# A two-layer encoder step on one core: the passages between dense blocks taken by token halves

## The chip, the core and the metric

The kernel runs on one core of a Trainium2 chip. The metric is the device time of one execution in microseconds (us). TensorE does the matmuls, VectorE and ScalarE read its results from PSUM and do the element-wise work, GpSimd takes a little of that, and SyncE issues most DMAs. In the profile's rows they are PE, DVE, ACT, POOL and SP; PEld is TensorE's weight load.

## What is computed

One inference step of two layers over 656 token columns (16 meta tokens and 512 prompt tokens, then 8 streams of 16). Each layer is, cut to what matters:

```python
h = rmsnorm(x, norm_mix_pre)
mix = token_mixers(h)                     # one input projection, attention and HGRN2 heads, one output projection
x = x + rmsnorm(mix, norm_mix_post)
h = rmsnorm(x, norm_ffn_pre)
u = h @ w_ffn_up                          # 1024 -> 2 * 2816
f = (silu(causal_conv3(u[:, :2816])) * u[:, 2816:]) @ w_ffn_down
x = x + rmsnorm(f, norm_ffn_post)
```

and after the second layer `y = rmsnorm(x, final_norm)`. Everything is float32; beside y, caches and states are returned.

## The kernel before

Activations lie transposed: features on 128 partitions, the 656 tokens along a row, and D = 1024 features are `KD` = 8 chunks `X[:, k, :]`. A PSUM tile has two banks; a tile's result puts tokens 0 to 327 into the first (half 0, or A) and 328 to 655 into the second (half 1, or B). There are four PSUM tiles: `G[0]` and `G[1]`, which dense tiles use in turn (tile number tt goes to `G[tt % 2]`), and `WA` and `WB`, which attention and the norms use.

**Dense products.** To keep float32 accuracy, every operand is split into a high and a low part (`Hh`, `Hl` of activations, `whi`, `wlo` of weights), and a product is three matmuls. `tile()` makes one output tile of 128 features: 8 chunks (11 for the down projection) of 3 matmuls for each half, so 48 or 66 matmuls of 328 columns. Weights come as a stream of pieces of 128x1024: SyncE loads a piece into one of two raw buffers, `w_high` on ScalarE and `w_low` on VectorE split it into one of three slots, and a slot is free when the last tile that used it has ended (`piece_end`).

**Passages.** Between two dense blocks lies a passage: the norm over all features needs the last tile, the residual needs the norm, and the next block needs the new X. There are three between blocks (layer 0's output projection into FFN, layer 0's FFN into layer 1's input projection, layer 1's output projection into FFN), and one at each end of the kernel. In a passage of before, with all 656 tokens at once:

- the squares of the last tiles are added up in `acc` by VectorE (`add_square`), TensorE adds over partitions by a plain float32 product with `ones` (`norm_sum`), and ScalarE makes the factor `R` (`rstd`: Ln and Exp);
- for each chunk k, VectorE writes tmp = Y * gain * R (`residual`, L1178 to L1188), GpSimd adds it to X (L317 to L321), ScalarE writes `Hh` and the square of X (`split_x`, L832 to L837), VectorE writes `Hl` (`rest_of_x`, L1167 to L1170), and TensorE does chunk k of the next block's first tile and, by `ones`, of the sum of squares (`square_sum`, L399 to L410);
- the norm before the block isn't applied to X: the factor `R` of that norm is multiplied into the tiles when VectorE reads them from PSUM. So the first tiles can run before that `R` is known, but can't be read.

Every engine has one instruction queue, worked off in the order in which it is written, and semaphores carry the dependences between engines; `tile_free(tt)` makes TensorE wait until the tile two before has been read. In FFN two up tiles make one unit: the gate tile in G[0] (times R, convolution, silu) and the value tile in G[1] (times R and the gate). FFN's first up tile is number 0 here; a block's fourth tile, tile 3, goes to G[1], which tile 1 must have left.

## Time and profile before

| what | value |
|---|---|
| time, median of 3 runs | 2143.87 us (2143.34 to 2146.22) |
| the profiled execution's own time | 2142.33 us |
| its span | 2140.5 us |
| TensorE busy | 1990.0 us, 93% |
| VectorE, ScalarE, GpSimd busy | 1144.7, 714.7, 167.7 us |
| mean granted TensorE clock | 0.946 of full speed |

The busy time of TensorE is a modelled one (its matmuls are pipelined), and the span is that of one execution, 1.8 us below its own time. Busy shares are averages over stages with different limits; a passage is read from the timeline.

### The profile page before, as it was taken

Reading aid. Unit: us, or ns where it says so; the run is one execution under the profiler, and the core shown is the slowest. Engines: PE = TensorE matmul, PEld = TensorE weight load, DVE = VectorE, ACT = ScalarE, POOL = GpSimd, SP = SyncE. Lnnn points to the kernel's source line nnn. Section 1 sums busy time; section 2 is a strip of 40 time slices with the busy share of each in tenths; the row PEclk is TensorE's granted clock in tenths of the full one; section 3 lists DMA queues with packets and bytes.
Section 4 is the critical chain, followed back from the end, with each engine's and each line's share of the span. In section 5 each row is a group of like instructions: output and inputs, shape, how many; then the busy total and the mean of one; then the engine's idle time right before and its main releaser. Section 6 shows DMA issues by size and latency. Waiting matters only on the chain.

```text
span 2140.5 us, 30609 instructions
## 1 busy us (share of the span) xinstructions
PE 1990.0 (93%) x12316; PEld 1803.3 (84%) x12316; DVE 1144.7 (53%) x1819; ACT 714.7 (33%) x1064; POOL 167.7 (8%) x145
## 2 busy tenths in 40 slices
PE   7999989899799999999799999898988999999995
PEld 6988866469699999999788888564787999999993
DVE  4777754332666515664456778452237663266535
ACT  4444334233422222222243444352234222222222
POOL 0000032300200000000100001332001000000002
PEclk9999988889899999999898999797999999999997
DMA  5111130131122222222121111302121222222211
GB/s 181 56 51 61 61 82 1 45 109 50 33 80 79 70 79 70 70 79 70 53 84 46 51 61 60 72 1 89 64 70 52 70 70 79 70 79 70 79 51 54
DMA packets 42045, 141.83 MB, mean 66 GB/s; under 512 B 4961, under 2 KB 6881, under 8 KB 41889
## 3 DMA queue, kind: packets, MB, share of 16 engines
q1 hardware_dynamic: 33248, 117.51, 16.8%
q10 hardware_dynamic: 8656, 22.37, 3.3%
q8 instruction: 98, 1.61, 0.3%
q14 instruction: 43, 0.34, 0.0%
HBM read 130.13 MB, written 8.65 MB: 65 GB/s over the span
## 4 chain that ended last, share of the span: by engine, by line
PE 78%; DVE 12%; ACT 7%; issue 1%; DMA 1%; ACTq 0%; SPq 0%; DVEq 0%; POOLq 0%; POOL 0%
PE G L384 62%; PE WA L384 8%; PE WB L384 5%; DVE tmp L1124 2%; DVE Hl L1124 2%; PE G L388 2%; DVE Y L1124 2%; DVE DE L1124 1%; ACT sq L800 1%; PE WB L388 1%; DVE Z L1124 1%; DVE wlo L1124 1%; ACT Y L800 1%; ACT whi L800 1%; ACT tmp L800 1%
## 5 line engine op out<-in xcount | busy, mean ns | idle before, releaser
L384 PE MATMUL G<-Hh,wlo 128*128 128x328 f32 x2304 | 742.6, 322 | 49.7 <-DVE Hl L1124 49.1
L384 PE MATMUL G<-Hh,whi 128*128 128x328 f32 x2304 | 728.7, 316 | 0.0
L384 PE MATMUL G<-Hl,whi 128*128 128x328 f32 x2304 | 722.1, 313 | 0.0
L384 PEld LDWEIGHTS G<-Hh,wlo 128*128 128x128 f32 x2304 | 439.1, 191 | 62.8 <-issue 60.4
L384 PEld LDWEIGHTS G<-Hh,whi 128*128 128x128 f32 x2304 | 438.7, 190 | 2.2 <-issue 0.8
L384 PEld LDWEIGHTS G<-Hl,whi 128*128 128x128 f32 x2304 | 439.2, 191 | 0.0
L800 ACT ACTIVATE whi<-wraw 128x1024 fp32r<-128x1024 f32 x192 | 203.6, 1061 | 557.1 <-PE G L384 540.6
L1124 DVE TENSOR_TENSOR wlo<-wraw,whi 128x1024 fp32r<-128x1024 f32 x192 | 235.3, 1225 | 246.7 <-ACT whi L800 239.0
L384 PE MATMUL G<-gl,whi 128*128 128x328 f32 x704 | 220.5, 313 | 0.0
L384 PE MATMUL G<-gh,whi 128*128 128x328 f32 x704 | 219.6, 312 | 0.0
L384 PE MATMUL G<-gh,wlo 128*128 128x328 f32 x704 | 219.6, 312 | 0.0
L321 POOL TENSOR_TENSOR X<-X,tmp 128x656 f32<-128x656 f32 x32 | 50.3, 1573 | 1292.8 <-DVE tmp L1124 1292.8
L384 PEld LDWEIGHTS G<-gh,whi 128*128 128x128 f32 x704 | 132.2, 188 | 0.0
L384 PEld LDWEIGHTS G<-gh,wlo 128*128 128x128 f32 x704 | 132.2, 188 | 0.0
L384 PEld LDWEIGHTS G<-gl,whi 128*128 128x128 f32 x704 | 132.1, 188 | 0.0
L1124 DVE TENSOR_TENSOR ax<-G,R 128x328 f32<-128x328 f32 x132 | 51.0, 386 | 150.8 <-PE G L384 147.3
L384 PEld LDWEIGHTS WA<-Z 128*128 128x128 f32 x576 | 70.8, 194 | 25.2 <-DVE Z L1124 17.8
L800 ACT ACTIVATE tmp<-cc 128x528 f32<-128x528 f32 x88 | 42.2, 480 | 143.3 <-DVE cc L1124 142.0
L384 PE MATMUL WA<-Z 128*128 128x64 f32 (+1 forms) x576 | 72.8, 273 | 15.8 <-DVE Z L1124 10.2
L1124 DVE SCALAR_TENSOR_TENSOR cc<-ax,cols,cc 128x672 f32<-128x672 f32 x88 | 80.9, 919 | 3.1
L384 PE MATMUL WA<-sq,ones 128*128 128x328 f32 x160 | 58.8, 498 | 14.5 <-ACT sq L800 9.6
L800 ACT ACTIVATE DE<-DE 128x512 f32<-128x512 f32 (+1 forms) x64 | 45.3, 707 | 67.7 <-DVE DE L1124 63.9
(203 smaller groups left out, 2302.8 us busy)
## 6 DMA issues: line engine op xcount, KB each, us to landing
wraw<-in_wstream SPq DMA_DIRECT2D x192, 512.0 KB, 3.3
ckT<-in_ckT SPq DMA_DIRECT2D x12, 512.0 KB, 4.2
ctok<-in_ctok SPq DMA_DIRECT2D x12, 512.0 KB, 3.4
S<-in_s ACTq DMA_DIRECT2D x8, 512.0 KB, 5.0
o_sst<-S ACTq DMA_DIRECT2D x8, 512.0 KB, 3.3
o_y<-Y ACTq DMA_DIRECT2D x8, 328.0 KB, 2.2
ckT<-in_ckT ACTq DMA_DIRECT2D x4, 512.0 KB, 4.2
ctok<-in_ctok ACTq DMA_DIRECT2D x4, 512.0 KB, 3.9
```

The costliest lines, as they stand in the source:

```text
L321: pool.tensor_tensor(X[:, k, :], X[:, k, :], tmp[:, k % 2, :], ALU.add).then_inc(S("x"), 1)
L384: return pe.matmul(out, lhsT, rhs, start=start, stop=stop, skip_group_check=True)
L388: return pe.transpose(out, in_, ident[0:n, 0:n])
L800: return act.activation(*args, **kw)
L1124: return kind(*args, **kw)
```

## The change

It takes the passages by token halves, in five parts.

1. **The last two tiles of a block** (`last_two`): TensorE makes half A of tile 6, half A of tile 7, then half B of tile 6 and half B of tile 7, where before it made tile 6 and then tile 7. It waits for both G tiles ahead of the first half. The norm's sum for half A (`norm_sum_a`) stands in the middle of tile 6's half B.
2. **The residual by halves** (`residual_half`): for half A and then for half B, and VectorE now does the addition to X too, in two instructions of 328 columns for each chunk (GpSimd's part is gone). `Hh`, the squares, `Hl` and the sum of squares are by halves too.
3. **The next block's first three tiles** (`first_two`): for half A, chunk by chunk, tiles 0 and 1; for half B the same, and beside them half A of tile 2, which goes to the spare PSUM tile `WB`; then half B of tile 2. Before, the three tiles ran one after the other in G[0], G[1], G[0], with the passage's chain beside the first alone.
4. **Weights**: the splits of the next block's first three pieces move from behind the passage into it, between the steps of half A.
5. **The ends**: the kernel's first tiles use the same order, and the last norm and the output are by halves too, with 16 output DMAs of half the size where there were 8.

The diff, cut (`A`, `B`, `AB` are slices of a half or both; semaphore bookkeeping is left out):

```diff
+        def PS(tt):
+            return WB if tt % TILES in (2, T_UP[0] + 2) else G[tt % 2]
-        NORM_SQ = [KD, 1, 1, 1, 2, 1, 1, KD, KD, KD]
+        NORM_SQ = [0, 1, 1, 1, 2, 1, 1, KD, 0, KD]
...
-            def residual(r):
-
-                for k in range(KD):
-                    pool.wait_ge(S("dx"), r * KD + k + 1)
-                    pool.tensor_tensor(X[:, k, :], X[:, k, :], tmp[:, k % 2, :], ALU.add).then_inc(S("x"), 1)
...
+            def square_half(i, x, k):
+                pe.wait_ge(S("sqh"), 2 * KD * i + KD * x + k + 1)
+                mm(bank(WA, x), ones[:, :], sq[:, k % 2, cols_of(x)], k == 0, k == KD - 1).then_inc(S("sqh_summed"), 1)
...
+            def last_two(tt, chunks, rh, rl, r):
+                n = len(chunks[0])
+                tile_free(tt)
+                tile_free(tt + 1)
+                half_tile(tt, chunks[0], rh, rl, 0, (0, n), "half_a")
+                half_tile(tt + 1, chunks[1], rh, rl, 0, (0, n), "half_a")
+                half_tile(tt, chunks[0], rh, rl, 1, (0, n // 2 + 1), None)
+                norm_sum_a(r, WA)
+                half_tile(tt, chunks[0], rh, rl, 1, (n // 2 + 1, n), "tile")
+                half_tile(tt + 1, chunks[1], rh, rl, 1, (0, n), "tile")
+
+            def first_two(tt, g, base, i, halves_free, between):
+                for x in range(2):
+                    if x:
+                        tile_free(tt)
+                        tile_free(tt + 1)
+                    elif halves_free:
+                        pe.wait_ge(S(halves_free[0]), halves_free[1])
+                    for k in range(KD):
+                        pe.wait_ge(S("hl"), base + KD * x + k + 1)
+                        for j in range(2):
+                            half_tile(tt + j, [(g + j, c * P, c) for c in range(KD)], Hh, Hl, x, (k, k + 1),
+                                      "tile" if x else None)
+                        if i == x == k == 0:
+                            pe.wait_ge(S("const"), 16 * N_CONST)
+                        square_half(i, x, k)
+                        between(x, k)
+                        if x:
+                            half_tile(tt + 2, [(g + 2, c * P, c) for c in range(KD)], Hh, Hl, 0, (k, k + 1), None)
+                half_tile(tt + 2, [(g + 2, c * P, c) for c in range(KD)], Hh, Hl, 1, (0, KD), "tile")
...
-                for n in range(2, KD):
+                for n in range(2, KD - 2):
                     out_tile(n)
-                norm_sum(n0 + N_MIXPOST, WA)
+                last_two(t0 + T_OUT + KD - 2, [[(g0 + P_OUT + n, k * P, k) for k in (4, 5, 6, 7, 0, 1, 2, 3)]
+                                               for n in (KD - 2, KD - 1)], Hh, Hl, 2 * l + 1)
+
+                def sum_mix_out(x, k):
+                    if not x and k == 5:
+                        norm_sum(n0 + N_MIXPOST, WA)
+                first_two(t0 + T_UP[0], g0 + P_UP[0], l * SPLITS + 2 * KD + 2, 2 * l + 1, ("evac_a", 2 * l + 2), sum_mix_out)
...
+            def split_xh(l, i, c_w, x, k):
+                did(f(Hh[:, k, cols_of(x)], X[:, k, cols_of(x)], ACT.Copy, scale=cols[:, l, c_w + k:c_w + k + 1]), "hh")
+                square_xh(i, x, k)
...
+                for n in (KD - 2, KD - 1):
...
+                    act.wait_ge(S("half_a"), 4 * l + n - KD + 3)
+                    act.wait_ge(S(sq_free(c)[0]), sq_free(c)[1])
+                    out_square(n, A, "sqa")
+                    out_copy(n, A, "evac_a")
+                rstd_post_a(2 * l + 1)
...
+                out_b(KD - 2)
+                w_high(l, SPL + P_OUT + KD - 2)
+                for x in range(2):
+                    for k in range(KD):
+                        act.wait_ge(S("x"), 4 * KD * l + KD * x + k + 1)
+                        split_xh(l, 2 * l + 1, C_FFNPRE, x, k)
+                        if not x and k == 2:
+                            out_b(KD - 1)
+                        if not x and k == 3:
+                            w_high(l, P_UP[0] + 2)
+                        if not x and k == KD - 2:
+                            rstd_post_b(2 * l + 1)
                 act.dma_start(cst[:, :], a["cst"][l]).then_inc(S("cst_in"), 16)
-                rstd(n0 + N_FFNPRE, WA, D, R)
+                rstd_pre(2 * l + 1)
...
+            def residual_half(l, c_w, x, then):
+                for k in range(KD + 1):
+                    if k < KD:
+                        t_ = tmp[:, k % 2, cols_of(x)]
+                        step(tt_(t_, Y[:, k, cols_of(x)], R[:, cols_of(x)], ALU.mult))
+                        did(stt(X[:, k, cols_of(x)], t_, col(l, c_w + k), X[:, k, cols_of(x)], ALU.mult, ALU.add), "x")
+                    if k:
+                        then(x, k - 1)
...
+                def rest_for_ffn(x, k):
+                    rest_of_xh(l, l * SPLITS + 2 * KD + 2, C_FFNPRE, x, k)
+                    if not x and k == 0:
+                        w_low(l, SPL + P_OUT + KD - 2)
+                    if not x and k == 1:
+                        add_square_b(n0 + N_MIXPOST, KD - 2)
+                    if not x and k == 4:
+                        add_square_b(n0 + N_MIXPOST, KD - 1)
+                    if not x and k == 5:
+                        w_low(l, P_UP[0] + 2)
+                residual_half(l, C_MIXPOST, 0, rest_for_ffn)
...
+                    if not x and k == 0:
+                        ffn_out_b(KD - 2)
+                        w_low(l + 1, 0)
+                    if not x and k == 2:
+                        add_square_b(n0 + N_FFNPOST, KD - 2)
+                    if not x and k == 1:
+                        w_low(l + 1, 1)
+                    if not x and k == 4:
+                        ffn_out_b(KD - 1)
+                    if not x and k == 5:
+                        add_square_b(n0 + N_FFNPOST, KD - 1)
+                    if not x and k == KD - 1:
+                        w_low(l + 1, 2)
...
+            for x in range(2):
+                act.wait_ge(S("sqh_summed"), 4 * KD * DEPTH + KD * (x + 1))
+                rstd_half(x, "rstd_end")
+            for x in range(2):
+                for k in range(KD):
+                    act.wait_ge(S("y_out"), KD * x + k + 1)
+                    act.dma_start(a["o_y"][k, :, cols_of(x)], Y[:, k, cols_of(x)]).then_inc(S("out"), 16)
```

`half_tile` is `tile()` for one half, 3 matmuls for each chunk; `rstd_post_a` and `rstd_post_b` are the two halves of `rstd` after a block; `rstd_pre`, ahead of the next block, makes both halves of R once both sums of squares are complete; `rest_of_xh` writes half of `Hl`; `ffn_out_b` adds half B of a down tile to Y; `add_square_b` adds half B of a square to `acc`.

## Rows read from the trace of the kernel before

**Rows 1.** Page, part 4: the chain that ended last, by engine.
```profile
PE 78%; DVE 12%; ACT 7%; issue 1%; DMA 1%; ACTq 0%; SPq 0%; DVEq 0%; POOLq 0%; POOL 0%
```

**Rows 2.** Windows: stretch, length, busy us of five engines, granted clock, DMA share, GB/s.
```profile
544.90:580.70 35.80, 20.92 (x85) 15.93 (x86) 26.11 (x17) 15.74 (x20) 12.60 (x8) 0.81 0.02 5
1049.30:1087.10 37.80, 21.78 (x85) 15.90 (x85) 27.63 (x19) 17.62 (x21) 12.59 (x8) 0.77 0.02 6
2100.70:2140.50 39.80, 15.81 (x36) 7.93 (x36) 25.56 (x18) 11.15 (x14) 12.55 (x8) 0.70 0.19 73
1064.20:1068.70 4.50, 4.50 (x12) 3.66 (x13) 4.19 (x4) 0.33 (x2) 1.77 (x2) 0.50 0.00 0
```

**Rows 3.** Timeline of VectorE, layer 0's passage into FFN: start, length, instruction.
```profile
549.72 5.59 DVE L1124 SCALAR_TENSOR_TENSOR tmp<-Y,cols,R 128x656 f32<-128x656 f32 x3 [3.15 <-ACT R L800]
...
555.41 2.25 DVE L1124 SCALAR_TENSOR_TENSOR Hl<-X,cols,Hh 128x656 fp32r<-128x656 f32 x1
...
585.00 0.18 DVE L1124 COPY ax<-cst 128x16 f32<-128x16 f32 x1
...
591.88 0.84 DVE L1124 TENSOR_TENSOR tmp<-G,tmp 128x656 f32<-128x656 f32 x1
```

**Rows 4.** Timeline of TensorE, the same passage; in brackets the idle time before.
```profile
544.58 0.31 PE L384 MATMUL G<-Hl,whi 128*128 128x328 f32 x1
546.62 1.37 PE L384 MATMUL WA<-acc,ones 128*128 128x328 f32 x4 [1.73 <-DVE acc L1124]
557.80 0.61 PE L384 MATMUL G<-Hh,wlo 128*128 128x328 f32 x1 [9.81 <-DVE Hl L1124]
...
577.59 1.26 PE L384 MATMUL WA<-sq,ones 128*128 128x328 f32 x4
...
579.59 1.26 PE L384 MATMUL WA<-sq,ones 128*128 128x328 f32 x4
```

**Rows 5.** Groups of instructions by form: busy us, mean ns of one, idle before.
```profile
L1124 DVE TENSOR_TENSOR wlo<-wraw,whi 128x1024 fp32r<-128x1024 f32 x192 | 235.3, 1225 | 246.7 <-ACT whi L800 239.0 <-DVEq L1124 0.7
...
L1124 DVE SCALAR_TENSOR_TENSOR cc<-ax,cols,cc 128x672 f32<-128x672 f32 x88 | 80.9, 919 | 3.1
...
L1124 DVE TENSOR_TENSOR Z<-Y,DE 128x328 f32<-128x328 f32 x64 | 32.1, 501 | 5.5 <-DVE DE L1124 0.9 <-ACT DE L800 0.5
...
L800 ACT ACTIVATE tmp<-cc 128x528 f32<-128x528 f32 x44 | 28.5, 648 | 142.0 <-DVE cc L1124 142.0
...
L800 ACT ACTIVATE Hh<-X,cols 128x656 fp32r<-128x656 f32 x32 | 27.0, 843 | 14.1 <-POOL X L321 11.9
...
L800 ACT ACTIVATE tmp<-cc 128x128 f32<-128x128 f32 x44 | 13.7, 311 | 1.4
...
L1124 DVE SCALAR_TENSOR_TENSOR st<-st,DE,WA 128x128 f32<-128x128 f32 x32 | 11.1, 347 | 3.4
```

**Rows 6.** Timeline of ScalarE: its read of output tile 5.
```profile
531.33 0.72 ACT L800 ACTIVATE Y<-G 128x656 f32<-128x656 f32 x1
```

**Rows 7.** Timeline of TensorE: the norm's sum after layer 0's FFN.
```profile
1051.91 2.56 PE L384 MATMUL WA<-acc,ones 128*128 128x328 f32 x4 [2.64 <-DVE acc L1124]
```

**Rows 8.** Timeline of VectorE: down tile 5, and layer 1's input tile 3.
```profile
1030.11 0.84 DVE L1124 TENSOR_TENSOR Y<-Y,G 128x656 f32<-128x656 f32 x1
...
1108.92 0.84 DVE L1124 TENSOR_TENSOR gate<-G,R 128x656 f32<-128x656 f32 x1 [4.83 <-PE G L384]
```

**Rows 9.** Timeline of ScalarE and its queue at the start of layer 1.
```profile
1088.14 0.75 ACT L800 ACTIVATE R<-R 128x656 f32<-128x656 f32 x1
...
1089.39 0.94 ACTq L876 DMA_DIRECT2D S<-in_s  x2
```

**Rows 10.** Timeline of TensorE: the first norm's sum, waiting for constants.
```profile
16.30 2.56 PE L384 MATMUL WA<-sq,ones 128*128 128x328 f32 x4 [4.92 <-DMA Y<-in_ind]
```

**Rows 11.** Timeline of VectorE: layer 0's input tile 3 is read.
```profile
56.39 0.84 DVE L1124 TENSOR_TENSOR gate<-G,R 128x656 f32<-128x656 f32 x1 [4.83 <-PE G L384]
```

**Rows 12.** Timeline of VectorE: the eight writes of the output.
```profile
2130.38 7.46 DVE L1124 SCALAR_TENSOR_TENSOR Y<-X,cols,R 128x656 f32<-128x656 f32 x8 [5.52 <-ACT R L800]
```

## The prediction on record

> **What bounds the kernel now.** I read the page's chain first: 78% of it is TensorE, 12% VectorE [rows 1]. So dense matmuls set most of the time, and the change leaves their number as it is. What it can win lies in the passages, so I took windows over them [rows 2]: 35.8 us from layer 0's output projection into FFN, 37.8 from its FFN into layer 1, 39.8 at the end. In the first TensorE is busy 20.9 us, and what it must do there is one tile and the norm sums. The tile is 7.2: tile 5 was read from 530.6 and tile 7 ended at 544.9 [rows 4, 6], 14.3 us for 96 matmuls, 0.15 each. A chunk with its sum of squares takes 2.00 us (two sums in a row, [rows 4]): six matmuls, 0.90, and two halves of 0.55.
>
> The timeline then shows why TensorE idles. VectorE starts the residual 4.8 us after the last tile, and its `Hl` takes 2.25 us beside GpSimd's addition [rows 3]; by the line through [rows 5] (below) it would be 0.90. TensorE waits 9.8 us [rows 4], and it comes back at half clock: 0.50 granted for 4.5 us at the same place of the next passage [rows 2].
>
> **Prices of half operations.** A `tensor_tensor` of 328 columns takes 0.50 us [rows 5]. For `scalar_tensor_tensor` the trace has 128 columns (0.35) and 672 (0.92), none of 328; the line between gives 0.56, which I take, with 0.35 and 0.92 as ends. ScalarE's 128 and 528 columns (0.31, 0.65) give 0.48, and 0.57 for half of `Hh` (0.84 less 0.27). With 0.16 us of gaps, a VectorE step (product, addition to X, `Hl`) is 1.78 us, and 1.12 without `Hl`. TensorE's step is 6 x 0.15 + 0.55 = 1.45 us in half A, and 1.90 in half B, where half a chunk of tile 2 joins it.
>
> **Passage into FFN, twice.** I follow layer 0's.
> - `last_two` waits for both G tiles: tile 5 is read until 532.05 [rows 6], and its successor's first matmul would have been due at 530.3. A loss of 1.8 us, in the place of nothing.
> - Halves A of tiles 6 and 7 to 539.35, five chunks and the sum to 542.15, half of R (two ScalarE operations) at 543.5. VectorE starts 6.2 us earlier than at 549.72 [rows 3].
> - Half A on VectorE: eight steps 14.2; two weight splits 2.65 (1.23 each, [rows 5]); two half additions to `acc` 1.2; a wait of 0.65 for the first `Hh`, which ScalarE writes behind tile 6's half B and a split; 1.0 at the end for the last `Hh`, which stands behind R's second half. To 563.3. Tile 7's half B ends at 547.3 beneath it, so TensorE follows VectorE.
> - Half B: two loop heads 2.2 and `Hl` 0.66 until TensorE can start, 566.3. Then TensorE is the slower one: 7 x 1.90 + 1.45, to 581.05.
> - Both halves of R cost four ScalarE operations, 2.15, and 0.3 to be seen: 583.5. Tile 2 is complete at 585.1. But tile 3 needs G[1], and tile 1 leaves it only after the first unit's convolution and silu: 7.8 us from VectorE's copy to its product with G [rows 3]. So tile 3 starts at 591.4. Before: 579.59 + 1.10 + two tiles = 595.1 [rows 4]. Won: 3.7 us.
> - The stall is new: 6.3 us without a matmul ahead of tile 3. After 9.8 us idle TensorE came back at half clock, after 2.64 too ([rows 7]: the four sums take 2.56), after 1.73 not (1.37, [rows 4]). At half clock it ran 4.5 us of work at 1.2 GHz [rows 2]; that costs half, 2.2 us. The 1.8 us ahead of `last_two` I leave without such a cost.
>
> The Trainium skill (TensorE: Matmul & The Clock Gate, Why this matters for your kernels) warns of idle gaps between matmul bursts, after which the clock is back at half. It speaks against this change, since the wait ahead of tile 3 is such a gap and did not exist. With the rule the passage wins 1.5 us, without it 3.7; the rows above say the same as the rule, and the sum goes by them.
>
> Net 1.5 us for each, 3.0 for both.
>
> **Passage into layer 1, once.** Tile 7 ended 2.64 us before 1051.91, at 1049.27 [rows 7]. Down tile 5 is read from 1030.11 for 0.84 and released near 1031.1 [rows 8], so `last_two` loses 1.85 us again. Halves A and six chunks (9.9 + 2.7), the sum and R: 1045.65. Half A on VectorE: 14.2, three splits 4.0, two half additions to Y with their marks 1.5, two to `acc` 1.2, waits 0.7 and 1.5: 1068.35. Half B reaches TensorE 2.9 later and takes 14.75: 1086.05; R at 1088.5 (before 1088.89, [rows 9]: nothing won there). What is won is that tiles 1 and 2 are nearly done. G[1] is free after three DMA issues on ScalarE's queue (to 1.4 us behind R, [rows 9]), piece 3's two splits and a product, 4.8 us: tile 3 runs from 1093.3 to 1100.7. Before, it was read at 1108.92 [rows 8]. Won 8.2, less 2.2 for the clock after a gap of 3.2: 6.0.
>
> **The start.** Constants hold the first sum until 16.30 [rows 10] before and after. Then 7 x 1.45 and 8 x 1.90, with 2.3 us more at half clock, put the last sum at 44.05 and R at 46.5, and the same 4.8 us free G[1] at 51.3. Tile 3 ends at 58.7, or 60.9 with the clock's cost; before 56.4 [rows 11]. A loss of 2.3 + 2.2 = 4.5. Before, R came under tile 1 and cost nothing.
>
> **The end.** `last_two` and the norm as above put half A's R at 2097.05 (layer 0's 1045.65 and the 1051.4 between the ends of the two down blocks, [rows 2]). Sixteen steps of 1.12, the additions 2.7 and a wait of 1.6 for half B's R end the residual at 2119.4; square, sum, R of the last norm: VectorE starts writing at 2121.0, two times 4.7 to 2130.5. The last DMA needs 2.7 us, as behind 2137.84 now [rows 12]: 2133.2. Sixteen issues of about 0.5 (two in 0.94, [rows 9]) keep that pace. Won 7.3. GpSimd's 50 us of additions cost nothing to remove and gain nothing but VectorE's undisturbed 0.90.
>
> **Sum.** 3.0 + 6.0 + 7.3 - 4.5 = 11.8 us off the profiled execution's 2142.33: 2130.5. The median of the runs shown is 1.5 above that execution, so 2132.
>
> **Rivals.**
> - *The clock stays up.* The gaps ahead of tile 3 would cost no restart: 4 x 2.2 = 8.8 less, 2123. For it: 1.73 us idle did no harm; against: 2.64 did, and all four of my gaps are 3.2 or more, by a sum with some slack.
> - *More slack than I count.* VectorE's 0.56 could be nearer 0.35, which makes the 24 steps with `Hl` 0.42 shorter and the 16 without 0.21: 13.4 less, 2118. Against: 328 columns of the sister operation cost 0.50.
> - *Nothing gained.* The third tile's weights are late or the work behind tile 3 waits for something else (a piece, layer 1's states), so that what is won before it is given back: only the end remains, less the start, 2139 to 2144. For it: piece 1's split comes 1 to 2.5 us late for TensorE by my sums; against: in layer 1, before, VectorE waited 4.83 us for tile 3 and for nothing else [rows 8].
> - *VectorE becomes the bound, slower.* A half `scalar_tensor_tensor` at 0.92, as if a whole one: a step is 2.50, 24 steps lose 0.72 and 16 lose 0.36, and half B's 24 fall behind TensorE's 1.90 by 0.6: 37 us more, 2169. It decides from a step of about 2.1 us, where the gain is gone; at 2.25 the time is near 2148. Against: 128 columns cost 0.35.
>
> The Trainium skill (SBUF — State Buffer, SBUF: two separate sides) says that GpSimd and a VectorE operation with two SBUF inputs take one port pair exclusively, so the loser blocks. If `Hl` beside GpSimd were slow for another reason, it would stay above 0.90 and this rival would gain; but eight such operations with GpSimd at rest take 7.46 us, 0.93 each [rows 12], so I weigh it little.
>
> **How the numbers follow.** The computed case 0.48 (own range 2126 to 2137), the clock staying up 0.20, more slack 0.12, nothing gained 0.12, slower 0.08. The range leaves out the slow case and the far part of the slack: 2116 to 2142. A measurement of this kernel can tell 0.2%, 4.3 us: faster means below 2139.6. The first three cases and a quarter of the fourth are faster, 0.83; same 0.10; slower 0.07.
>
> **What the profile after would show.** Right: no POOL addition in the passages; half operations of 0.50 and 0.56 on VectorE; TensorE idle for about 6 us ahead of tile 3 in FFN and 3 us at layer 1 and at the start, with 0.5 granted behind it; tile 3 in FFN starting at 591.4, now 595.1; the span's end 30 us behind the last down tile, now 39.8. Wrong: half-B steps slower than 1.90, or tile 3 starting right behind tile 2, which would mean that G[1] comes free sooner than I have it.

## The result, and the profile after

The changed kernel takes 2129.81 us, median of 5 runs (2125.24 to 2140.77), beside 2143.87 for the kernel before: a ratio of 0.9936, with a 95% interval of 0.9907 to 0.9965. Twelve further runs beside seventeen of the kernel before gave 0.9957 (0.9935 to 0.9979). So the gain is 9 to 14 us, where 12 were predicted. Its profiled execution took 2126.35 us with a span of 2124.5 (before: 2142.33 and 2140.5).

I follow the passages by marks that every version has: VectorE's or ScalarE's read of tile 5 ahead of a passage, and VectorE's read of tile 3 behind it. In the kernel before these are the reads at 1030.11 and 1108.92 [rows 8] for the passage into layer 1, and from 530.57 (its read's second half is [rows 6]) to 602.49 for the one into FFN. The start counts from 0 to the read of input tile 3, the end from the read of down tile 5 to the end of the span. Rows of the kernel before for three of its marks (ScalarE's read of output tile 5, VectorE's reads of FFN's tile 3 and of the last down tile 5):

```profile
530.57 0.72 ACT L800 ACTIVATE sq<-G 128x656 f32<-128x656 f32 x1 [4.56 <-PE G L384]
...
602.49 0.84 DVE L1124 TENSOR_TENSOR tmp<-G,tmp 128x656 f32<-128x656 f32 x1 [0.49 <-PE G L384]
...
2081.54 0.84 DVE L1124 TENSOR_TENSOR Y<-Y,G 128x656 f32<-128x656 f32 x1
```

| us | start | into FFN, layer 0 | into layer 1 | into FFN, layer 1 | end |
|---|---|---|---|---|---|
| before | 56.4 | 71.9 | 78.8 | 71.9 | 59.0 |
| after | 59.6 | 71.0 | 73.6 | 71.5 | 51.4 |
| won | -3.2 | 0.9 | 5.3 | 0.5 | 7.5 |
| predicted | -4.5 | 1.5 | 6.0 | 1.5 | 7.3 |

The passages give 10.9 us of the 16.0 between the two spans; the FFN blocks between them are alike (427.6 us in all four). The other 5 us lie in the attention stretches, whose instructions the change leaves as they are; I come back to them.

Windows of the trace after: layer 0's passage from the read of tile 5 to TensorE's first matmul of half B, then the end passage, the restart ahead of tile 3 in layer 1's mixer, and the same in FFN (columns as in [rows 2]).

```profile
526.93:562.90 35.97, 29.45 (x164) 24.78 (x165) 22.36 (x38) 20.32 (x37) 0.00 (x0) 1.00 0.14 44
2073.06:2124.50 51.44, 34.28 (x168) 26.02 (x168) 31.58 (x58) 15.65 (x30) 0.00 (x0) 0.88 0.16 57
1088.00:1094.00 6.00, 3.92 (x19) 3.92 (x20) 3.99 (x4) 1.89 (x2) 0.00 (x0) 0.80 0.91 333
588.00:598.00 10.00, 9.80 (x50) 9.81 (x51) 8.35 (x15) 2.77 (x4) 0.00 (x0) 0.74 0.31 98
```

The fifth of the busy columns is GpSimd: nothing of it is left in the passages, where [rows 2] had 12.6 us each. In the last two, behind the gaps ahead of tile 3, the clock is below 1.

VectorE's groups of layer 0's passage into FFN after, by form, from 539 to 581 us:

```profile
L1272 DVE SCALAR_TENSOR_TENSOR X<-tmp,cols,X 128x328 f32<-128x328 f32 x16 | 9.0, 560 | 0.6
L1272 DVE SCALAR_TENSOR_TENSOR Hl<-X,cols,Hh 128x328 fp32r<-128x328 f32 x16 | 8.9, 559 | 3.6 <-ACT Hh L864 1.8 <-DVE X L1272 0.5
L1272 DVE TENSOR_TENSOR tmp<-Y,R 128x328 f32<-128x328 f32 x16 | 8.0, 500 | 3.5 <-ACT R L864 2.9
```

The half scalar_tensor_tensor takes 0.56 us, the value interpolated in the prediction. TensorE's timeline has the three stalls: ahead of last_two, ahead of half B, ahead of tile 3. For the first the profile names no releaser (`<-issue`); e1_late_free shows what it is.

```profile
528.50 0.39 PE L381 MATMUL G<-Hh,wlo 128*128 128x328 f32 x1 [1.60 <-issue]
...
562.91 0.39 PE L381 MATMUL G<-Hh,wlo 128*128 128x328 f32 x1 [1.51 <-DVE Hl L1272]
...
588.20 0.64 PE L381 MATMUL G<-Hh,wlo 128*128 128x328 f32 x1 [6.21 <-DVEq L1272]
588.63 0.47 PE L381 MATMUL G<-Hh,whi 128*128 128x328 f32 x1
```

A matmul of 0.47 is one at half clock (0.31 at full). Tile 3 waits for G[1]. VectorE's product that frees it starts at 587.19 and ends 7.7 us behind the start of the copy that opens VectorE's first unit (the prediction had 7.8). Tile 3 is read 9.8 us after its first matmul, where a tile at full clock is 7.2:

```profile
539.84 0.50 DVE L1272 TENSOR_TENSOR tmp<-Y,R 128x328 f32<-128x328 f32 x1 [2.91 <-ACT R L864]
...
580.31 0.18 DVE L1272 COPY ax<-cst 128x16 f32<-128x16 f32 x1
...
587.19 0.84 DVE L1272 TENSOR_TENSOR tmp<-G,tmp 128x656 f32<-128x656 f32 x1
...
597.96 0.84 DVE L1272 TENSOR_TENSOR tmp<-G,tmp 128x656 f32<-128x656 f32 x1 [0.67 <-PE G L381]
```

### The profile page after: what moved, and what is told of

Same layout as the page of the kernel before. It is cut to its first block, busy times and chain, and to the rows that moved or that the text cites. A ratio compares the mean times of both kernels' runs of the same rounds, so it can differ in the third digit from the quotient of the medians.

```text
span 2124.5 us, 30928 instructions
## 1 busy us (share of the span) xinstructions
PE 1989.3 (94%) x12316; PEld 1800.7 (85%) x12316; DVE 1152.5 (54%) x1967; ACT 739.5 (35%) x1166; POOL 117.7 (6%) x113
## 3 DMA queue, kind: packets, MB, share of 16 engines
q8 instruction: 98, 1.61, 0.3%
## 4 chain that ended last, share of the span: by engine, by line
PE 79%; DVE 11%; ACT 8%; issue 2%; DMA 1%; ACTq 0%; DVEq 0%; SPq 0%
PE G L381 61%; PE WA L381 8%; PE WB L381 6%; DVE Y L1272 1%; PE G L385 1%; DVE tmp L1272 1%; DVE wlo L1272 1%; DVE DE L1272 1%; PE WB L385 1%; ACT sq L864 1%; DVE X L1272 1%; ACT whi L864 1%; ACT Y L864 1%; DVE Z L1272 1%; ACT R L864 1%
## 5 line engine op out<-in xcount | busy, mean ns | idle before, releaser
L381 PE MATMUL G<-Hh,wlo 128*128 128x328 f32 x2240 | 723.4, 323 | 50.7 <-DVE Hl L1272 22.1
L381 PE MATMUL G<-Hh,whi 128*128 128x328 f32 x2240 | 710.0, 317 | 0.0
L381 PE MATMUL G<-Hl,whi 128*128 128x328 f32 x2240 | 703.9, 314 | 0.0
L381 PEld LDWEIGHTS G<-Hh,wlo 128*128 128x128 f32 x2240 | 428.8, 191 | 69.4 <-DVE Hl L1272 26.9
L381 PEld LDWEIGHTS G<-Hh,whi 128*128 128x128 f32 x2240 | 428.2, 191 | 1.1 <-issue 0.2
L381 PEld LDWEIGHTS G<-Hl,whi 128*128 128x128 f32 x2240 | 428.4, 191 | 0.0
L1272 DVE TENSOR_TENSOR ax<-G,R 128x328 f32<-128x328 f32 (+2 forms) x126 | 48.7, 386 | 150.2 <-PE G L381 147.1
L381 PEld LDWEIGHTS WA<-Z 128*128 128x128 f32 x576 | 71.9, 196 | 25.3 <-DVE Z L1272 16.1
L328 POOL TENSOR_TENSOR S<-S,dec 128x1024 f32<-128x1024 f32 x8 | 15.2, 1899 | 1086.9 <-PE WA L381 1086.8
L864 ACT ACTIVATE sq<-G 128x256 f32<-128x256 f32 (+3 forms) x52 | 27.9, 537 | 105.4 <-PE G L381 79.2
```

The source lines that it names most:

```text
L328: pool.tensor_tensor(s3, s3, dec[:, :].rearrange("p (b a) -> p b a", a=1).broadcast_to([P, DB, P]), ALU.mult).then_inc(S("s0_decayed"), 1)
L381: return pe.matmul(out, lhsT, rhs, start=start, stop=stop, skip_group_check=True)
L864: return act.activation(*args, **kw)
L1272: return kind(*args, **kw)
```

## The experiments

Every version has a profile; the marks above were read in each. In brackets the read of tile 5, where it says more than tile 3's. "Attention" is from the read of input tile 3 to that of output tile 5.

| us | start | FFN, layer 0 | layer 1 | FFN, layer 1 | end | attention 0, 1 |
|---|---|---|---|---|---|---|
| before | 56.4 | 71.9 (86.3) | 78.8 | 71.9 (86.3) | 59.0 | 474.2, 473.1 |
| before, again | 57.2 | 71.9 (86.3) | 78.3 | 72.0 (86.4) | 58.5 | 474.1, 470.0 |
| after | 59.6 | 71.0 (85.4) | 73.6 | 71.5 (85.9) | 51.4 | 467.3, 474.8 |
| after, again | 57.6 | 71.1 (85.5) | 73.6 | 71.5 (85.9) | 51.5 | 464.8, 474.8 |
| e1_late_free | 60.2 | 69.1 (83.5) | 70.0 | 68.9 (83.3) | 49.4 | 466.5, 474.8 |
| e2_no_third | 63.6 | 70.3 (84.7) | 74.5 | 69.9 (84.3) | 51.4 | 466.4, 476.2 |
| e3_warm | 57.6 | 70.5 (83.2) | 72.0 | 70.6 (83.3) | 51.4 | 463.8, 479.9 |
| e4_tile3_wa | 55.6 | 70.4 (80.6) | 69.4 | 70.4 (80.6) | 51.5 | 473.9, 478.7 |
| e5_pool_add | 60.0 | 75.9 (90.3) | 77.0 | 76.0 (90.4) | 53.7 | 476.9, 470.6 |
| e6_wa_late | 55.5 | 68.5 (79.3) | 68.7 | 68.6 (79.4) | 49.5 | 473.9, 476.0 |
| e7_relax | 55.6 | 68.5 (78.7) | 67.3 | 68.6 (78.8) | 49.4 | 470.8, 474.9 |
| e8_vec_whole | 55.8 | 66.7 (81.1) | 72.4 | 66.7 (81.1) | 53.2 | 469.5, 474.9 |
| e9_whole_third | 53.7 | 68.5 (79.1) | 70.8 | 68.6 (78.8) | 54.3 | 474.4, 471.5 |

**e1_late_free.** The later wait for tile 7's buffer.

```
                 tile_free(tt)
-                tile_free(tt + 1)
                 half_tile(tt, chunks[0], rh, rl, 0, (0, n), "half_a")
+                tile_free(tt + 1)
```

> Edit: in last_two, TensorE waits for tile 7's PSUM buffer only behind half A of tile 6, not ahead of it. Nothing is left out. Theory (the prediction's term of 1.8 us: tile 6 could run while tile 5 is still being read): the idle time ahead of last_two, 1.60 to 1.76 us in the profile after at each of the four passages, goes to under 0.3, half A's factor R comes 1.5 to 1.8 us earlier (layer 0: its first half 538.8 in the profile after, now 26.4 us behind the start of tile 5's read of ScalarE in place of 28), and each passage ends 1.5 to 1.8 us earlier, since VectorE's half A hangs on that factor and TensorE's half B on VectorE: 6 to 7 us less in all, about 2120 at the profile of after's 2126. Rival: TensorE would wait for the same reads a tile later (half A of tile 7 has only 3.6 us more), or half B of the residual is what sets the end and it does not move: then the wait moves behind half A of tile 6 and the passages stay at 71.0, 73.6, 71.4 and 51.4 us within 0.3.

Measured: 2119.18 us, ratio 0.9903 (0.9869 to 0.9937). The stall ahead of last_two is gone, and the passages are 1.9, 3.6, 2.5 and 2.0 us shorter. The term of 1.8 is confirmed. What layer 1's has beyond it, some 1.7, is the clock. In after TensorE fell to half clock behind the 2.81 us wait ahead of half B, about half a microsecond after it had restarted at full speed; the shares of 0.67 and 0.65 below, over 2 and 3 us, cost 1.7. In e1_late_free the wait is 2.80 and the clock stays up:

```profile
1067.00:1069.00 2.00, 1.95 (x9) 1.77 (x9) 1.82 (x4) 0.98 (x2) 0.00 (x0) 0.67 0.04 8
1069.00:1072.00 3.00, 3.00 (x14) 2.69 (x12) 2.69 (x6) 1.04 (x2) 0.00 (x0) 0.65 0.00 0
```

(windows of after), against (windows of e1_late_free)

```profile
1062.90:1065.00 2.10, 2.09 (x12) 1.93 (x13) 1.91 (x4) 1.29 (x3) 0.00 (x0) 1.00 0.03 8
1065.00:1068.00 3.00, 3.00 (x21) 2.74 (x19) 2.71 (x5) 1.73 (x4) 0.00 (x0) 1.00 0.00 0
```

**e2_no_third.** Tile 2 not beside half B.

```
-            return WB if tt % TILES in (2, T_UP[0] + 2) else G[tt % 2]
+            return G[tt % 2]
...
-                        if x:
-                            half_tile(tt + 2, [...], Hh, Hl, 0, (k, k + 1), None)
-                half_tile(tt + 2, [...], Hh, Hl, 1, (0, KD), "tile")
```

> Edit: tile 2 of the next block is not computed beside half B in spare PSUM banks; tiles 0 and 1 alone are, and tile 2 follows whole in G[0]. Nothing is left out. Theory (tile 3 waits for G[1], which needs the factor R and 4.8 to 7.8 us of VectorE and ScalarE behind it, so what the third tile won is idle time ahead of tile 3): half B on TensorE runs at VectorE's pace of 1.79 us a chunk in place of 1.90, R comes 0.8 us earlier, tile 2 in G[0] waits for the read of tile 0 (R + 3 to 5 us), then tile 3 for G[1] at R + 7.8; the passage into FFN ends within 1 us of after's 71.0 (tile 2 and 3 then follow one another: R + 4 + 7.2 + 7.2 = R + 18.4 for both, against R + 7.8 + 7.2 + 2.3 = R + 17.3 in after), the one into layer 1 2 to 4 us later than 73.6 (there G[1] is free at R + 4.8, tile 3 ends at R + 12.5 in after), the start 2 to 4 us later. Sum: 5 to 10 us more than after, 2132 to 2136. Rival (the third tile is the whole gain of the change, 7.2 us of TensorE work at each of four places): each passage ends 7 us later, the time is that of before or above, 2145 to 2155.

Measured: 2128.51 us, ratio 0.9950 (0.9931 to 0.9969). The time is that of after, below the 2132 to 2136 that I had expected. Without the third tile the passages into FFN are *shorter* by 0.8 and 1.6 us, the one into layer 1 is 1.0 longer, the start 4 to 6 longer (59.6 and 57.6 in after's two profiles). So in FFN, where tile 3 waits 7.8 us behind R, a tile computed ahead of it buys idle time; the rival, 7 us at each place, is out.

**e3_warm.** Matmuls that nobody reads fill the gap ahead of tile 3.

```
                 half_tile(tt + 2, [...], Hh, Hl, 1, (0, KD), "tile")
+                pe.wait_ge(S("rstd"), i // 2 * N_NORM + (N_FFNPRE if i % 2 else N_MIXPRE) + 1)
+                for _ in range(10 if i % 2 else 3):
+                    mm(bank(WA, 0), ones[:, :], X[:, 0, cols_of(0)])
```

> Edit: behind tile 2 of the next block TensorE waits for the factor R and then runs dummy matmuls in plain fp32 into a PSUM bank that nobody reads then, ten in the passages into FFN and three at the layers' starts, so that the 6.2 us gap ahead of tile 3 is filled; they add work and leave none out. Theory (the clock): tile 3 took 9.7 us in after from its first matmul to its read at the passages into FFN, where 7.2 is a tile at full clock; with the gap filled it starts at the same time and takes 7.2 to 7.4, so the passages into FFN end 2.3 us earlier, and the others, whose gap of 2.4 us cost 0 to 2.3, 0 to 2 us: 5 to 7 less in all, about 2120. Rival (the slow tile 3 comes from something else, its weights or Hh and Hl contended by the same reads, or the dummies hold TensorE beyond the moment when G[1] is free): tile 3 takes 9.7 us again or starts later by what the dummies overhang, and the sum does not fall, 2126 to 2132.

Measured: 2121.96 us, ratio 0.9924 (0.9898 to 0.9949). TensorE's timeline of e3_warm: the ten dummies (two records each) fill 5.68 us, the gap is 0.69 us and tile 3 runs at full clock.

```profile
576.24 5.68 PE L381 MATMUL WA<-X,ones 128*128 128x328 f32 x20
582.60 0.42 PE L381 MATMUL G<-Hh,wlo 128*128 128x328 f32 x1 [0.69 <-DVEq L1275]
582.86 0.31 PE L381 MATMUL G<-Hh,whi 128*128 128x328 f32 x1
583.00 0.31 PE L381 MATMUL G<-Hl,whi 128*128 128x328 f32 x1
```

Tile 3 is read only 0.5 us earlier in layer 0 and 0.9 in layer 1, since VectorE isn't ready for it; tile 5 is read 2.2 and 2.6 us earlier, tile 3 of layer 1's mixer 1.5. So the clock's cost in FFN is real and of the size predicted, 2.2, but VectorE, still busy with the unit before, hides most of it at tile 3.

**e4_tile3_wa.** Tile 3 in the sum's PSUM banks.

```
-            return WB if tt % TILES in (2, T_UP[0] + 2) else G[tt % 2]
+            return WB if tt % TILES in (2, T_UP[0] + 2) else WA if tt % TILES in (3, T_UP[0] + 3) else G[tt % 2]
...
-                if lo == 0:
+                if lo == 0 and PS(tt) is WA:
+                    pe.wait_ge(S("rstd"), ...)
+                elif lo == 0:
                     tile_free(tt)
...
+                w_high(l, P_UP[0] + 3)
                 rstd_pre(2 * l + 1)
```

> Edit: tile 3 of the next block goes to the two PSUM banks that hold the norm's sums, which are free as soon as the factor R is computed, and no longer to G[1]; the split of its weights moves ahead of that factor on ScalarE and on VectorE. Nothing is left out. Theory (the prediction's 7.8 us from R to G[1] free is what holds tile 3): tile 3 starts at R + 0.1 to 0.3 or right behind tile 2, the gap of 6.2 us falls under 1, the clock stays full and the tile takes 7.2 in place of 9.7. From tile 3's start 6 us and the clock's 2.3 are won at each passage into FFN, less what tiles 4 and 5 then wait for G[0] and G[1] (their readers take 5 to 6 us per pair): 5 to 8 us each there, 2 to 4 us into layer 1 and at the start; 14 to 20 us in all, 2106 to 2112. Rival (VectorE's and ScalarE's chain of readers, not TensorE, sets the passage: they read tiles 0 to 3 at the same times as before): tile 3 starts early but tiles 4 and 5 wait as long as tile 3 did, and the passages stay within 1 us of 71.0, 73.6 and 71.4, the time at 2124 to 2130.

Measured: 2109.86 us, ratio 0.9866 (0.9842 to 0.9890). The gap ahead of tile 3 is gone and tile 5 is read 4.9 and 5.3 us earlier. Tile 3 itself is read hardly earlier (70.4): VectorE now runs its units back to back, 10.2 us each, and is the bound for three of them. The new stall is ahead of tile 4, which goes to G[0]:

```profile
594.50 0.42 PE L381 MATMUL G<-Hh,wlo 128*128 128x328 f32 x1 [2.65 <-DVE ax L1277]
```

It ends with VectorE's read of tile 2, which lies in WB. TensorE waits for a buffer that nobody uses, since the count of reads goes by the tile's parity.

**Both kernels again**, c_before and c_after.

> The kernel before as it is, profiled once more: how far do its own stretches repeat? Theory: the passages and the start repeat (71.9, 78.8, 71.9 and 59.0 us within 0.3, the start within 3 by its transfers), and the attention stretches, 474.18 and 473.06 in the first profile of it, come out anywhere between 463 and 480, as those of the changed kernel and its variants did. Rival: the kernel before has 474 and 473 again within 1 us, and the changed kernel's layer 0, 467.3 and 464.8, owes its lower value to the change.

> The changed kernel as it is, profiled and timed once more beside the others. Question: in the first profile of it the stretch of layer 0 between the read of input tile 3 (59.60) and the read of output tile 5 (526.93) took 467.33 us where the kernel before took 474.18, though the change touches nothing there; layer 1's took 474.84 where 473.06 stood. Theory (the clock in the attention stage differs from execution to execution: granted 0.88 between 200 and 300 us before, 0.95 after): the stretch comes out anywhere between 463 and 476 us and the passages repeat within 0.3 us (start 59.6, 71.0, 73.6, 71.4, end 51.4). Rival (the shifted start systematically changes how the stretch runs): 467.3 within 1 us again.

Measured: 2139.12 us (one run) and 2128.71. Neither expectation held whole: the passages repeat within 0.5 us, not 0.3, the start within 2, and attention repeats within 0.1 us in two pairs and within 2.5 and 3.1 in the others: 474.2 and 474.1 before, 467.3 and 464.8 after in layer 0; 473.1 and 470.0 before, 474.8 twice after in layer 1. The granted clock goes the same way: from 300 to 520 us 0.87 in both profiles before, 0.89 and 0.90 after; from 1140 to 1350 0.94 and 0.96 before, 0.93 twice after. By these four profiles the change would win 7 to 9 us in the one and lose 2 to 5 in the other, though it edits nothing there. But e5_pool_add (below), which is the changed kernel instruction for instruction up to layer 0's first residual, has 476.9 in layer 0 and 470.6 in layer 1, with granted clocks of 0.87 and 0.95 in the same windows. So the code doesn't fix these stretches, and the 5 us that attention gave between the two profiles are not shown to be the change's. The other versions lie between 464 and 480 without an order that I could tie to an edit. What sets the clock there stays open.

**e5_pool_add.** The halves kept, the additions back on GpSimd.

```
-                        step(tt_(t_, Y[:, k, cols_of(x)], R[:, cols_of(x)], ALU.mult))
-                        did(stt(X[:, k, cols_of(x)], t_, col(l, c_w + k), X[:, k, cols_of(x)], ALU.mult, ALU.add), "x")
+                        did(stt(tmp[:, k % 2, cols_of(x)], Y[:, k, cols_of(x)], col(l, c_w + k), R[:, cols_of(x)],
+                                ALU.mult, ALU.mult), "dx")
...
+                        pool.tensor_tensor(X[:, k, cols_of(x)], X[:, k, cols_of(x)], tmp[:, k % 2, cols_of(x)],
+                                           ALU.add).then_inc(S("x"), 1)
```

> Edit: the additions to X go back to GpSimd, in halves of 328 tokens: VectorE writes Y times weight times R into tmp (one scalar_tensor_tensor, 0.56 us), GpSimd adds it to X, and Hh, Hl and the square follow; everything else is as in the changed kernel. Nothing is left out. Theory (the prediction: GpSimd's additions go for VectorE's undisturbed operations; Hl took 2.25 us beside one of 656 tokens, 0.90 without): a step without contention would be 0.56 + 0.56 and gaps, 1.3 us; with it Hl takes 1.1 to 1.6 us, the step 1.8 to 2.3 us in place of 1.79, and the chain X, Hh, Hl gets one hand-over more. Half A of the residual (539.8 to 559.1 for its last Hl in the changed kernel, 19.2 us) takes 19 to 24, the end passage (no Hl, steps 1.12 there) gets longer by what GpSimd needs for half an addition, about 0.8 us beyond VectorE's pace at most: passages 71 to 76, end 51 to 54, in all 2126 to 2145. Rival (moving the additions to VectorE was no gain, the halves alone are): with 0.5 us less work on VectorE per step the passages are the same or shorter by up to 4 us each, the time 2115 to 2126.

Measured: 2147.04 us, one run; the passages are 4.8, 3.4, 4.5 and 2.2 us longer than after's, and those into FFN 4 us longer than in the kernel before. The time is 2 us above my range; attention is 5 us longer here than in after's first profile. VectorE's timeline of e5_pool_add shows why, with GpSimd's beside it:

```profile
555.73 0.56 DVE L1282 SCALAR_TENSOR_TENSOR tmp<-Y,cols,R 128x328 f32<-128x328 f32 x1
556.39 1.21 DVE L1282 SCALAR_TENSOR_TENSOR Hl<-X,cols,Hh 128x328 fp32r<-128x328 f32 x1
...
568.16 0.56 DVE L1282 SCALAR_TENSOR_TENSOR Hl<-X,cols,Hh 128x328 fp32r<-128x328 f32 x1
```

```profile
556.37 0.88 POOL L327 TENSOR_TENSOR X<-X,tmp 128x328 f32<-128x328 f32 x1 [2.43 <-DVE tmp L1282]
```

`Hl`, which starts with the addition, ends 0.35 us after it and takes 1.21; with GpSimd at rest it takes 0.56. The Trainium skill (SBUF — State Buffer, SBUF: two separate sides) says that the two share a port pair as an exclusive lock and the loser blocks for the whole instruction. An estimate by that rule is 0.88 of waiting and 0.56 of its own, 1.44; in the trace `Hl` does end behind the addition, but it takes 1.21, so less than that.

**e8_vec_whole.** The reverse, made of the kernel before: the additions move, nothing is halved.

```
-                    if k < KD:
-                        if k >= 2:
-                            dve.wait_ge(S("x"), r * KD + k - 1)
-                        did(stt(tmp[:, k % 2, :], Y[:, k, :], col(l, c_w + k), R[:, :], ALU.mult, ALU.mult), "dx")
+                    if k < KD:
+                        step(tt_(tmp[:, k % 2, :], Y[:, k, :], R[:, :], ALU.mult))
+                        did(stt(X[:, k, :], tmp[:, k % 2, :], col(l, c_w + k), X[:, k, :], ALU.mult, ALU.add), "x")
```

> Edit of the kernel before: the additions to X move from GpSimd to VectorE, over all 656 tokens (a tensor_tensor, 0.84 us, and a scalar_tensor_tensor with the addition, 0.90), and nothing else of the change is made: no halves, no third tile, no early split. Nothing is left out. Theory (GpSimd's share of the change's gain is large: in the trace of e5_pool_add a half Hl takes 1.22 us beside GpSimd's addition and 0.56 without, and the passages into FFN are 4.8 us longer): a step with Hl takes 0.84 + 0.90 + 0.90 + 0.16 = 2.80 us in place of 3.36, eight of them win 4.5 us at each of the passages into FFN and into layer 1, and 8 x (2.35 - 1.84) = 4 at the end: 17 us in all, 2124 by the kernel's median of about 2141, as much as the whole change. Rival (the prediction's: the additions cost nothing to remove and give back only the undisturbed Hl, the gain is in the halves): a passage loses the three products that ran ahead of the additions and the longer first chunk and wins 0 to 2 us, the whole 2136 to 2142.

Measured: 2123.41 us (2109.43 to 2136.31), ratio 0.9916 (0.9886 to 0.9945). By the traces this one part of the change wins more than the whole: the passages into FFN are 66.7 us (before 71.9, after 71.0), the one into layer 1 72.4, and the start is unhurt; only the end, 53.2, is longer than after's 51.4. Against before the passages are 5.2, 6.5, 5.3 and 5.7 us shorter, 22.7 in all. The times alone would not show it: the median is 5 to 6 us below after's, but the intervals of the two ratios overlap. And the profiled execution, 2116.25, is 7 us below its median: by medians e8_vec_whole wins 18 us, less than its passages and start (23). Where the other executions lose that isn't traced. VectorE's groups, first of before from 549 to 578 us, then of e8_vec_whole from 544 to 567.5:

```profile
L1124 DVE SCALAR_TENSOR_TENSOR Hl<-X,cols,Hh 128x656 fp32r<-128x656 f32 x8 | 15.3, 1914 | 0.8
L1124 DVE SCALAR_TENSOR_TENSOR tmp<-Y,cols,R 128x656 f32<-128x656 f32 x8 | 9.9, 1244 | 3.8 <-ACT R L800 3.1
```

```profile
L1116 DVE SCALAR_TENSOR_TENSOR X<-tmp,cols,X 128x656 f32<-128x656 f32 x8 | 7.2, 902 | 0.3
L1116 DVE SCALAR_TENSOR_TENSOR Hl<-X,cols,Hh 128x656 fp32r<-128x656 f32 x8 | 7.2, 901 | 0.8
L1116 DVE TENSOR_TENSOR tmp<-Y,R 128x656 f32<-128x656 f32 x8 | 6.7, 842 | 3.4 <-ACT R L792 3.1
```

VectorE takes over GpSimd's work and still has less to do: 25.2 us before, 21.1 now.

**e6_wa_late and e7_relax.** The two waits together, and then tiles 4 and 5 by their own buffer:

```
+                early = tt % TILES in (4, 5, T_UP[0] + 4, T_UP[0] + 5)
                 if tt >= 2:
-                    pe.wait_ge(S(f"evac{tt % 2}"), slot_use(tt) - 1)
+                    pe.wait_ge(S(f"evac{tt % 2}"), slot_use(tt) - 1 - early)
```

> Edit: e1_late_free and e4_tile3_wa together: tile 7's buffer is waited for behind half A of tile 6, and tile 3 of the next block goes to the sum's PSUM banks with its weights split ahead of R. Nothing is left out. In the traces of the two alone, measured between the read of the tile before the passage and the read of tile 5 of the next block, the first took 1.9 and 2.5 us off the passages into FFN, 3.6 off the one into layer 1 and 2.0 off the end; the second 4.9 and 5.3 (6 with the tiles behind), 4.2 and, at the start, 2.7. Theory (both lie one behind the other on the same path): they add, 10 + 19 us, 27 to 30 us below the changed kernel, 2098 to 2104, ratio to the kernel before about 0.980. Rival (VectorE bounds the FFN units behind the passage, 10.2 us a unit in the trace of e4_tile3_wa, and takes part of it back): 20 to 24 us, 2105 to 2110.

> Edit: e6_wa_late, and tiles 4 and 5, which now follow a tile that doesn't lie in their G buffer, wait for the reads of tiles 0 and 1 (their buffer's last users) and no longer for those of tiles 2 and 3. Nothing is left out. Theory (the gap of 2.65 and 2.69 us ahead of tile 4 in the trace of e4_tile3_wa ends with VectorE's read of tile 2 in WB, which doesn't free G[0]): TensorE goes on without a gap, tiles 4 and 5 are read at most 2.7 us earlier, and the FFN block behind is bound by TensorE, so each passage into FFN wins 2.7 us, the other two nothing: 5.4 us below e6_wa_late, about 2095. Rival (VectorE's unit of 10.2 us sets the pace behind the passage, not TensorE): the gap only moves to tile 6 or later, each passage wins 0 to 1 us, and the time is that of e6_wa_late within 2 us.

Measured: e6_wa_late 2110.67 us, 0.9862 (0.9837 to 0.9888), just above the rival's range and far from the theory's. From the read ahead of the passage to that of tile 7, where TensorE has caught up, it takes 93.7 us in layer 0, e4_tile3_wa 94.1 and after 99.8: the 1.8 us don't add while VectorE is the bound. e7_relax: 2097.27 us, 0.9805 (0.9778 to 0.9832), the best version. There the same stretch is 89.8, and TensorE idles only 0.26 us in 42 (window 578 to 620 of e7_relax, then of after):

```profile
578.00:620.00 42.00, 41.74 (x278) 41.50 (x278) 35.50 (x57) 15.57 (x20) 0.00 (x0) 1.00 0.28 90
```

```profile
578.00:620.00 42.00, 35.79 (x224) 35.52 (x223) 28.05 (x45) 15.16 (x21) 0.00 (x0) 0.92 0.23 76
```

I had expected 2.7 us per passage into FFN from it, and 3.9 came; of the 13.5 us between the spans of the two versions 7.9 are these, 1.4 lie in the passage into layer 1 and 4.2 in the attention stretches. The rival saw rightly that tiles 1, 3 and 5 are read no more than 0.6 us earlier (VectorE's pace); what counts is tile 7.

**e9_whole_third.** The same PSUM layout with whole tokens.

```
+            def first_pair(tt, g, base, n):
+                for k in range(KD):
+                    for j in range(2):
+                        tile(tt + j, [...], Hh, Hl, lambda k: pe.wait_ge(S("hl"), base + k + 1), (k, k + 1))
+                    square_sum(n, k)
```

> Edit: e8_vec_whole (whole tokens, additions on VectorE) with the PSUM layout of e7_relax and no halves at all: tile 1 runs chunk by chunk beside tile 0 behind VectorE's residual, tile 2 follows at once in WB, tile 3 in the sum's banks behind R with its weights split ahead of R, tiles 4 and 5 wait for the reads of tiles 0 and 1. The last two tiles of a block and the end are as in the kernel before. Nothing is left out. Theory (halving a passage wins nothing: in the trace of e8_vec_whole eight whole steps take 22.5 us where sixteen half steps take 28.6, and the 6.1 us more eat the earlier start of 6.2; the gain of e7_relax is in PSUM buffers for tiles 2 and 3): TensorE needs 2.9 us a chunk against VectorE's 2.82, the splits ahead of R cost 2 to 3 us, the reads of tiles 1, 3, 5 come at 58, 68, 79 us behind the read of output tile 5 as in e7_relax within 1.5 us, the passage into layer 1 takes 67 to 70, only the end (53.2 against 49.4) stays longer: 2097 to 2104. Rival (the halves are what e7_relax lives on, because TensorE has work under half A): the passages are 3 us or more longer than in e7_relax, 2108 to 2120.

Measured: 2111.30 us, 0.9856 (0.9831 to 0.9880). The reads of tiles 1, 3 and 5 come where they do in e7_relax, within 0.4 us, as my theory had it, but that of tile 7 comes 3.4 us later (93.2 against 89.8), the passage into layer 1 is 3.5 longer and the end 4.9. TensorE, idle 6.5 us ahead of its first chunk here, then works without a stop until tile 7 is read (68.98 us of 68.98, from 552.02 in layer 0): it starts too late and is the bound. Only the start is shorter, by 1.9. My theory that halving wins nothing falls for this layout: the time is the rival's.

## Why the prediction was right, point by point

The number was right, 2132 against 2130 and 2129, and so was the mechanism; no term is off by more than 1.3 us against the first profile. That the passages' sum comes so close, 11.8 against 10.9 (12.8 between the second profiles), is in part errors that cancel: the start and the end came out 1.5 us better, the three passages between them 2.3 worse. The profiled execution was 4 us faster than the 2130.5 forecast for it, and that was attention, which the prediction leaves as it is.

- *Half operations*: 0.50 and 0.56, exact; 1.79 us a step (predicted 1.78), 1.90 in half B.
- *The path through layer 0's passage*, from tile 5's read (530.57 before, 526.93 after): VectorE starts 12.9 us behind it (predicted 12.9), TensorE's half B at 36.0 (35.7), the last sum's reader at 51.0 (50.5), tile 3 at 61.3 (60.8), after an idle time of 6.2 (6.3).
- *The 1.8 us of last_two*: 1.60 to 1.76 idle, and taking the wait away gave 1.9 to 2.5 at three places (e1_late_free).
- *The clock behind the gap*: half for the beginning of tile 3, in FFN at once, in layer 1's mixer 1.5 us after the restart. e3_warm won 2.2 and 2.6 us on tile 5's read, as predicted. The Trainium skill's rule on idle gaps (TensorE: Matmul & The Clock Gate, Why this matters for your kernels) holds for the gaps of 6.2; about gaps of 2.4 to 2.8 the traces differ, as e1_late_free and the start show. The rival that the clock stays up is out for FFN and layer 1, but at the start it came true in one of the two profiles.
- *The start* lost 3.2 and 0.4 us in two profiles, where 4.5 were predicted. The gap ahead of tile 3 is 2.37 and 2.36, not 3.2 or more, and behind it the clock was at half in the first profile and at full in the second (rows in the last section). So the term of 2.2 for the clock is right in one execution and nothing in the other.
- *The passage into layer 1* won 5.3 (4.7 between the second profiles), predicted 6.0. Here the sum lacks a term: TensorE fell to half clock in half B too (e1_late_free), so R was ready at 60.3 us behind the read of tile 5 and not at 58.4. G[1] came free 4.2 us behind R in place of 4.8, and tile 3 took 9.06 in place of 7.4 + 2.2. VectorE's rows of after:

```profile
1025.59 0.84 DVE L1272 TENSOR_TENSOR Y<-Y,G 128x656 f32<-128x656 f32 x1
...
1085.85 0.84 DVE L1272 TENSOR_TENSOR Y<-G,R 128x656 f32<-128x656 f32 x1 [5.21 <-ACT R L864]
...
1099.14 0.84 DVE L1272 TENSOR_TENSOR gate<-G,R 128x656 f32<-128x656 f32 x1 [3.72 <-PE G L381]
```

  The prediction also added wrongly here: 1045.65 and its terms for half A make 1068.75, not 1068.35, and with that 5.6 would have been forecast.
- *The end* won 7.5 (7.0), predicted 7.3.
- *The passages into FFN* won 0.9 and 0.5, predicted 1.5 each.
- *More slack* and *VectorE as the bound* were excluded by the 0.56. (The latter's price for a step of 2.25 us was added up wrongly: by its own terms it is some 23 us, so 2155 and not 2148.) *Nothing gained* had one fact right, piece 1's split is late: TensorE waits 1.61 us for it ahead of tile 1 in layer 1's passage. It is not to be seen in the time: TensorE's half B starts 41.5 us behind the read of tile 5, as the sum put right has it, since VectorE's half A is the bound there.

One sentence of the prediction was misleading, though it costs the sum nothing: that GpSimd's additions "cost nothing to remove and gain nothing but VectorE's undisturbed 0.90". That undisturbed time was folded into the half steps and credited to the halves. e8_vec_whole separates them: moving the additions wins 22.7 us in the passages, and the halves, the third tile and the early split on top of it lose 12.3 (4.3 and 4.8 in FFN, 1.2 into layer 1, 3.8 at the start, less 1.8 at the end; 2 us of the start's are the clock and missing in after's second profile). With e5_pool_add the table has all four corners, as sums of the start, the passages and the end: before 338.0, the additions alone 314.8, the rest alone 342.6, both 327.1.

The reason: in layer 0's passage VectorE starts 6.2 us earlier behind the read of tile 5, but its residual takes 34.6 us (539.84 to 574.44) where e8_vec_whole's takes 22.5 (544.46 to 566.98). Of the 12.1 us more, 6.1 are the halves' own, sixteen steps of 1.79 against eight of 2.82, as the prediction's numbers would have told. The other 6 are two weight splits and two additions to `acc`, which e8_vec_whole has outside its residual, and three waits of 0.46 to 0.98 us that it doesn't have. So the lead is spent, and nearly 6 us more. Part of that comes back, because one split less stands behind R. The third tile, beside half B, only lengthens FFN's wait for G[1] (e2_no_third). What the early splits alone are worth was not run.

What halving does buy is work for TensorE under half A, and that is worth something once PSUM lets the tiles behind follow: from e9_whole_third to e7_relax it is 3.4 and 3.3 us on the passages into FFN (read of tile 7) and 3.5 into layer 1, less 1.9 at the start. At the end, where no tile follows, halving wins in either layout: 1.8 us from e8_vec_whole to after, 4.9 from e9_whole_third to e7_relax, of which 2.0 are the later wait of e1_late_free and 1.0 is the clock. So in the passages between blocks it is the same idea with opposite signs. Between the two pairs lie the later wait for tile 7's buffer, tile 3's place with its early split and the wait of tiles 4 and 5; how much of the turn each of them makes was not separated.

## What to carry to other kernels

Where a change has several parts that share an operation's duration, price each part alone on the kernel before: here the part that looked like housekeeping was worth more than the whole. Ahead of doing a tile early, ask which buffer the tile after it waits for; if that one is freed by a chain behind the same norm, as G[1] in FFN, the early tile buys only idle time and a clock at half. And count reads by the buffer and not by the tile's parity as soon as one tile lies elsewhere.

## What the hardware showed unasked

- TensorE restarted at full speed after a gap of 2.37 us and fell to half 1.5 us later (TensorE's timeline of after; 0.31 us a matmul, then 0.48):

```profile
1090.08 0.41 PE L381 MATMUL G<-Hh,wlo 128*128 128x328 f32 x1 [2.37 <-DVE Y L1272]
...
1091.40 0.33 PE L381 MATMUL G<-Hl,whi 128*128 128x328 f32 x1
1091.56 0.45 PE L381 MATMUL G<-Hh,wlo 128*128 128x328 f32 x1
1091.80 0.48 PE L381 MATMUL G<-Hh,whi 128*128 128x328 f32 x1
```

  So a first matmul at full speed doesn't say that a gap was free; the tile took 9.06 us to its read.
- A gap of the same length at the same place can cost the clock in one execution and not in another. Ahead of tile 3 at the start, the changed kernel's first profile and its second; then the norm's sum at the end, e9_whole_third and e8_vec_whole, whose code there is the same (each time the clock is at half in the first and full in the second):

```profile
50.61 0.64 PE L381 MATMUL G<-Hh,wlo 128*128 128x328 f32 x1 [2.37 <-DVE Y L1272]
51.05 0.48 PE L381 MATMUL G<-Hh,whi 128*128 128x328 f32 x1
```

```profile
50.09 0.42 PE L381 MATMUL G<-Hh,wlo 128*128 128x328 f32 x1 [2.36 <-DVE Y L1272]
50.34 0.31 PE L381 MATMUL G<-Hh,whi 128*128 128x328 f32 x1
```

```profile
2076.38 2.39 PE L380 MATMUL WA<-acc,ones 128*128 128x328 f32 x4 [2.64 <-DVE acc L1135]
```

```profile
2082.95 1.37 PE L376 MATMUL WA<-acc,ones 128*128 128x328 f32 x4 [2.64 <-DVE acc L1116]
```

  The gaps of 2.80 and 2.81 us in e1_late_free's section are a third pair, with one edit between them. So the prediction's reading that 2.64 us cost the clock [rows 7] is one of two outcomes. The gaps of 6.2 us and more in FFN always came back at half.
- Beside GpSimd's addition VectorE's `Hl` loses 0.65 us per half operation and 1.35 per whole one (1.21 against 0.56; 2.25 in [rows 3] against 0.90).
